# Last chunk of a second MLP: token-major output with the squared-relu part stationary and the weights moving

## The chip, the cores and the metric

The kernel runs on one core of one Trainium2 chip. The metric is the device time of the whole kernel in microseconds (us), as the median of the runs.

## The reference, cut to what matters

The reference computes two transformer blocks over 512 tokens with 1024 features. The change touches only the very end: the last quarter of the second block's MLP, its residual addition, and the final norm.

```
def squared_relu_mlp(u, w_ff1, w_ff2):       # u (512, 1024), w_ff1 (1024, 4096), w_ff2 (4096, 1024)
    hdn = jnp.square(jax.nn.relu(jnp.einsum('bld,df->blf', u, w_ff1)))
    return jnp.einsum('blf,fd->bld', hdn, w_ff2)
...
    h = h + squared_relu_mlp(rmsnorm_2(h, norm_ffn[l]), w_ff1[l], w_ff2[l])
    return rmsnorm_2(h, norm_final)[:, N_META:]
# rmsnorm_2(x, g) = x * rsqrt(mean(x * x, over features) + 1e-6) * g
```

## The kernel before, in words

All activations are held feature-major: `X[p, m, token]` holds feature 128m+p. Column 0 to 15 are meta tokens, 16 to 527 (`META:S2`) the 512 real ones. Every dense product is made of **slabs**: one slab is 128 output features for all 512 tokens, with the weight tile (128x128) stationary and the activations (128x512) moving. For precision each operand is split into a high part in a reduced format and a low part (the remainder), and three products are summed: high by high, high by low, low by high. With eight tiles of the contraction a slab is 24 matmuls. Slabs have a running number `t`.

Five engines work through hand-written streams and meet in counting semaphores:

- **SP** issues the weight loads (`load(p)`, L484 to L491; in the MLP's loop L504). One load brings 1 MB, the raw weights of two slabs, into one of the two halves of `raw`. `load(p)` waits until the low parts of load p-2 were made (`lo_ready`), so two loads ahead are possible.
- **ACT** makes the high part of slab t+2's weights (`wh`, L717 or L666) when slab t is done, because `wh` and `wl` have two slots.
- **DVE** makes the low part (`wl`, L1144 or L1073) and then increments `lo_ready`.
- **TensorE** (PE) starts slab t when `lo_ready` is above t and the result of slab t-2 is evacuated (`evac_done`), because results alternate between two PSUM banks (`products`, L1710; `mlp_chunk`, L1743).

Each MLP has four **chunks** of 1024 hidden features. A chunk is eight slabs of the first product (`j` 0 to 7) and eight of the second (`j` 8 to 15). In the first eight, DVE multiplies the result by the norm's factor `RS` (L1153), makes relu times itself (L1155), ACT copies the high part of the hidden value (L724), and DVE takes the low part (L1158). The second MLP keeps it in `Bh` and `Bl`. In the order of the code, both engines first convert slab t+2's weights and then treat slab t. In the second eight, DVE adds the result to `X` (L1129). Three chunks run in a hardware loop; the last is unrolled (`last`). Its loads come from L531 and L532.

In the last chunk of the second MLP the second eight slabs also prepare the final norm: ACT squares the new `X` (L679) and makes `Y`, `X` times the gain (L745); GpSimd sums the squares (L579), DVE the last one (L1085). TensorE turns `Y` to token-major with four 128x128 transposes for each m (`turn_y`, L1765), into four banks; after m = 3 ACT copies the first halves out (L751). After the last slab come the last square, the sum over partitions by four small matmuls (L2178), mean and epsilon (L1682), square root (L1053), reciprocal (L1684), and the scaling of the four token blocks, the right halves on ACT (L1057) and the left ones on DVE (L1688). SP writes the block of each 128 tokens when both halves are there (L537).

The waits that set the order of loads, and the order of an ACT and DVE step:

```
L488                    sp.wait_ge(lo_ready, loads[p - 2][4] + loads[p - 2][3])
L531            for p in range(second_mlp + 8 * (CHUNKS - 1), len(loads)):
L532                load(p)
L1152                        dve.wait_ge(slab_done, t + 16 * c + 1)
L1748                    pe.wait_ge(lo_ready, t + 16 * c + 1)
L1749                    pe.wait_ge(evac_done, t + 16 * c - 1)
```

Of the kernel before, what the change touches and what calls it, by code (L numbers as in the profile page):

```python
# [32 lines left out]
P = 128  # L33
# [136 lines left out]
def build(nc, d):  # L170
# [21 lines left out]
    with ctx:  # L192
# [152 lines left out]
        y_ready, y_psum, y_copied, y_low, y_high, out_done = (  # L345
            sem("y_ready"), sem("y_psum"), sem("y_copied"), sem("y_low"), sem("y_high"), sem("out_done"))
# [43 lines left out]
        def lr_slab(col):  # L390

            return w_slab(wh, T2_LR % 2, KT)[:, :, col:col + 16]

# [71 lines left out]
        def _(sp):  # L465
# [76 lines left out]
        def _(pool):  # L542
# [103 lines left out]
            add_squares(4, REAL)  # L646
# [3 lines left out]
        def _(act):  # L650
# [51 lines left out]
            def mlp_chunk(which, c, last):  # L702
                t0, n0, p0 = MLPS[which]
                w = width(which)
                for j in range(16):
# [16 lines left out]
                    if j < 8:  # L722
                        act.wait_ge(f_ready, staged(n0) + 8 * c + j)
                        act.activation(HIDDEN[which][0][:, j, 0:w], F[:, (n0 + j) % 2, 0:w], ACT.Copy)\  # L724
                           .then_inc(hi_split, 1)
                    elif last:
                        m = j - 8
                        act.wait_ge(evac_done, t + 16 * c + 1)
                        square(2 if which == ONE else 4, m, which)
                        if which == ONE:  # L730

                            x = X[:, m, META:S2]
                            if m >= 2:
                                act.wait_ge(ss2_done, m - 1)
                            else:
                                act.wait_ge(gain2_ready, 1)
                            act.activation(SQ2[:, m % 2, :], x, ACT.Square, scale=vecT[:, G_FIN + m:G_FIN + m + 1])\
                               .then_inc(sq2_ready, 1)
                            act.activation(Bh[:, m, META:S2], x, ACT.Copy, scale=gain2[:, m:m + 1])\
                               .then_inc(hi_split, 1)  # L740
                            if m == 0:
                                act.activation(Bh[:, :, 0:META], meta2, ACT.Copy).then_inc(meta_hi, 1)
                        else:

                            act.activation(Y[:, m, :], X[:, m, META:S2], ACT.Copy,  # L745
                                           scale=vecT[:, G_FIN2 + m:G_FIN2 + m + 1]).then_inc(y_ready, 1)
                            if m == 4:

                                act.wait_ge(y_psum, 4)
                                for a in range(4):  # L750
                                    act.activation(ON[:, a, 0:512], ps[:, Y_BANKS[a], :], ACT.Copy)\  # L751
                                       .then_inc(y_copied, 1)
# [3 lines left out]
            def mlp(which):  # L756
                with act.Fori(0, CHUNKS - 1) as c:
                    mlp_chunk(which, c, False)
                mlp_chunk(which, CHUNKS - 1, True)
# [292 lines left out]
            act.wait_ge(ms_ready, 5)  # L1052
            act.activation(r_tok, r_tok, ACT.Sqrt).then_inc(sqrt_ready, 1)  # L1053
            act.wait_ge(rstd_ready, 5)
            act.wait_ge(y_psum, KT)
            for a in range(4):
                act.activation(ON[:, a, 512:1024], ps[:, Y_BANKS[a], :], ACT.Copy, scale=r_tok[:, a:a + 1])\  # L1057
                   .then_inc(y_high, 1)
# [3 lines left out]
        def _(dve):  # L1062
# [69 lines left out]
            def mlp_chunk(which, c, last):  # L1132
                t0, n0, p0 = MLPS[which]
                w = width(which)
                for j in range(16):
# [24 lines left out]
                    else:  # L1160
                        add_residual(t + 16 * c, t, j - 8, which)
                        if last:
                            m = j - 8
                            if m == KT - 1:
                                add_square(2 if which == ONE else 4, m, which)
                            if which == ONE:

                                if m == KT - 1:
                                    dve.wait_ge(sq2_ready, KT)
                                    dve.wait_ge(ss2_done, m)  # L1170
                                    dve.wait_ge(meta_sum, 1)
                                    dve.tensor_tensor(SS2[:, META:S2], SS2[:, META:S2], SQ2[:, m % 2, :], ALU.add)\
                                       .then_inc(ss2_done, 1)
                                dve.wait_ge(hi_split, N2_MIX + m + 1)
                                dve.scalar_tensor_tensor(out=Bl[:, m, META:S2], in0=X[:, m, META:S2],
                                                         scalar=gain2[:, m:m + 1], in1=Bh[:, m, META:S2],
                                                         op0=ALU.mult, op1=ALU.subtract).then_inc(act_ready, 1)
                                if m == 0:
                                    dve.wait_ge(meta_hi, 1)
                                    dve.tensor_tensor(Bl[:, :, 0:META], meta2, Bh[:, :, 0:META], ALU.subtract)\  # L1180
                                       .then_inc(meta_split, 1)
# [3 lines left out]
            def mlp(which):  # L1185
                with dve.Fori(0, CHUNKS - 1) as c:
                    mlp_chunk(which, c, False)
                mlp_chunk(which, CHUNKS - 1, True)
# [492 lines left out]
            dve.wait_ge(stat_done, 5)  # L1681
            dve.tensor_scalar(r_tok, ps[:, 7, 0:4], 1.0 / DM, EPS, ALU.mult, ALU.add).then_inc(ms_ready, 1)  # L1682
            dve.wait_ge(sqrt_ready, 5)
            dve.reciprocal(r_tok, r_tok).then_inc(rstd_ready, 1)  # L1684
            dve.wait_ge(rstd_ready, 5)
            dve.wait_ge(y_copied, 4)
            for a in range(4):
                dve.tensor_scalar(ON[:, a, 0:512], ON[:, a, 0:512], r_tok[:, a:a + 1], None, ALU.mult)\  # L1688
                   .then_inc(y_low, 1)
# [3 lines left out]
        def _(pe):  # L1693
# [49 lines left out]
            def mlp_chunk(which, c, last):  # L1743

                t0, n0, _ = MLPS[which]
                for j in range(1, 16 if last else 17):
# [9 lines left out]
                    if last and which == REAL and j >= 9:  # L1756
                        turn_y(j - 9)

            def turn_y(m):

                pe.wait_ge(y_ready, m + 1)
                if m == 4:
                    pe.wait_ge(y_copied, 4)
                for a in range(4):
                    mm = pe.transpose(ps[:, Y_BANKS[a], (m % 4) * P:(m % 4 + 1) * P], Y[:, m, a * P:(a + 1) * P],  # L1765
                                      ident[:, :])
                mm.then_inc(y_psum, 1)

            def mlp(which):
# [5 lines left out]
                mlp_chunk(which, CHUNKS - 1, True)  # L1775
# [400 lines left out]
            pe.wait_ge(ss_done, 8 * 4)  # L2176
            for a in range(4):
# [27 lines left out]
```

## Time and profile before

| | |
|---|---|
| median of 3 runs | 1458.56 us (1457.64 to 1458.94) |
| profiled execution, its own time | 1457.75 us |
| its span, first to last instruction | 1456.0 us |
| mean granted TensorE clock | 0.998 of full speed |
| TensorE busy | 1440.0 us, 99% |
| VectorE (DVE) busy | 776.1 us, 53% |
| ScalarE (ACT) busy | 503.8 us, 35% |
| GpSimd (POOL) busy | 79.1 us, 5% |
| moved by DMA | 130.58 MB, mean 90 GB/s |

The profiled execution has a span and, outside of it, 1.75 us of start and end. Times in rows are counted from the span's start. An engine with a low share of busy time can still be waited for: what counts is what ends each wait of the engine that bounds. PE's weight loads (PEld) run beside its matmuls, and the duration of one matmul in a row is longer than the distance from one to the next, because they are pipelined.

### The profile page before, as it was taken

To read this page: it belongs to the slowest core of one execution; us is meant where nothing else is said; L and a number is where in the kernel's file an instruction comes from. 1 tells how busy PE (TensorE), PEld (TensorE's weight loads), DVE (VectorE), ACT (ScalarE), POOL (GpSimd) and SP (SyncE) were. 2 spreads that over 40 slices of the span, in tenths; PEclk is the share of its full clock that TensorE was granted. 3 is DMA by queue.
4 is the path that set the end of the run, shared out by engine and by line. 5 is a ranking of instruction groups with operands and counts; after the bars stand their busy time and mean duration, and the time that the engine had idled before them with its cause. 6 is when DMAs were issued, how large, how long until landed. Compare 5 with 4: busy or idle time off the path is not lost.

```text
span 1456.0 us, 18718 instructions
## 1 busy us (share of the span) xinstructions
PE 1440.0 (99%) x7726; PEld 1161.2 (80%) x7726; DVE 776.1 (53%) x971; ACT 503.8 (35%) x705; POOL 79.1 (5%) x101
## 2 busy tenths in 40 slices
PE   8999999999999999999999999999999999999997
PEld 7887778777888888888878987777888888888885
DVE  5535433666665354453556787555756345353442
ACT  5224532554433122231343444343442222122233
POOL 4000000000110000000031210000010000000001
PEclk9999999999999999999999999999999999999999
DMA  5223122111233223222323222232233223223321
GB/s 177 87 89 107 59 86 88 59 59 52 93 96 101 93 86 109 93 86 91 112 81 92 74 66 87 75 100 87 87 96 107 87 90 112 86 86 97 105 87 58
DMA packets 125349, 130.58 MB, mean 90 GB/s; under 512 B 2282, under 2 KB 122452, under 8 KB 125284
## 3 DMA queue, kind: packets, MB, share of 16 engines
q1 hardware_dynamic: 124756, 129.12, 27.5%
q8 instruction: 49, 0.80, 0.2%
q10 hardware_dynamic: 528, 0.52, 0.1%
q14 instruction: 16, 0.13, 0.0%
HBM read 126.75 MB, written 2.10 MB: 88 GB/s over the span
## 4 chain that ended last, share of the span: by engine, by line
PE 96%; DVE 2%; ACT 1%; DMA 0%; issue 0%; ACTq 0%; SPq 0%; DVEq 0%
PE ps L1710 85%; PE ps L1706 4%; PE ps L1963 1%; PE ps L1990 1%; PE ps L1976 1%; PE ps L2079 1%; DVE wl L1144 0%; PE ps L1867 0%; DMA arena<-in_norm_mix_g 0%; PE ps L1843 0%; PE ps L1908 0%; PE ps L1887 0%; PE ps L2161 0%; PE ps L1926 0%; DVE wl L1073 0%
## 5 line engine op out<-in xcount | busy, mean ns | idle before, releaser
L1710 PE MATMUL ps<-Ah,wh 128*128 128x512 f32 x1008 | 401.4, 398 | 2.4 <-DVE wl L1234 2.1
L1710 PE MATMUL ps<-Al,wh 128*128 128x512 f32 x1008 | 398.5, 395 | 0.0
L1710 PE MATMUL ps<-Ah,wl 128*128 128x512 f32 x1008 | 396.7, 394 | 0.0
L1710 PE MATMUL ps<-Bh,wh 128*128 128x512 f32 x800 | 317.0, 396 | 0.2 <-issue 0.2
L1710 PE MATMUL ps<-Bl,wh 128*128 128x512 f32 x800 | 316.4, 395 | 0.0
L1710 PE MATMUL ps<-Bh,wl 128*128 128x512 f32 x800 | 314.6, 393 | 0.0
L717 ACT ACTIVATE wh<-raw 128x1024 fp32r<-128x1024 f32 x124 | 131.2, 1058 | 290.3 <-PE ps L1710 290.3
L1144 DVE TENSOR_TENSOR wl<-raw,wh 128x1024 fp32r<-128x1024 f32 x124 | 156.0, 1258 | 139.4 <-ACT wh L717 138.9
L1710 PEld LDWEIGHTS ps<-Ah,wh 128*128 128x128 f32 x1008 | 189.4, 188 | 49.9 <-DVE wl L1234 2.8
L1710 PEld LDWEIGHTS ps<-Ah,wl 128*128 128x128 f32 x1008 | 189.6, 188 | 43.2
L1710 PEld LDWEIGHTS ps<-Al,wh 128*128 128x128 f32 x1008 | 189.2, 188 | 42.3 <-issue 0.5
L666 ACT ACTIVATE wh<-raw 128x1024 fp32r<-128x1024 f32 (+2 forms) x129 | 120.4, 933 | 215.3 <-PE ps L1710 205.0
L1710 PEld LDWEIGHTS ps<-Bh,wh 128*128 128x128 f32 x800 | 150.3, 188 | 38.0 <-issue 1.4
L1710 PEld LDWEIGHTS ps<-Bh,wl 128*128 128x128 f32 x800 | 150.5, 188 | 34.2
L1710 PEld LDWEIGHTS ps<-Bl,wh 128*128 128x128 f32 x800 | 150.1, 188 | 34.0 <-issue 0.2
L1073 DVE TENSOR_TENSOR wl<-raw,wh 128x1024 fp32r<-128x1024 f32 (+2 forms) x129 | 142.4, 1104 | 36.2 <-ACT wh L666 35.7
L1129 DVE TENSOR_TENSOR X<-X,ps 128x512 f32<-128x512 f32 x64 | 44.0, 687 | 162.0 <-PE ps L1710 162.0
L1109 DVE TENSOR_TENSOR arena<-ps,RS 128x512 f32<-128x512 f32 (+2 forms) x59 | 40.7, 690 | 88.6 <-PE ps L1710 83.2
L724 ACT ACTIVATE Ah<-F 128x512 fp32r<-128x512 f32 x32 | 20.2, 632 | 85.6 <-DVE F L1155 85.6
L724 ACT ACTIVATE Bh<-F 128x512 fp32r<-128x512 f32 x32 | 20.2, 632 | 85.6 <-DVE F L1155 85.6
L1153 DVE TENSOR_TENSOR F<-ps,RS 128x512 f32<-128x512 f32 x64 | 43.8, 685 | 4.1 <-PE ps L1710 4.1
L1155 DVE SCALAR_TENSOR_TENSOR F<-F 128x512 f32<-128x512 f32 x64 | 44.3, 692 | 2.2
(261 smaller groups left out, 1047.3 us busy)
## 6 DMA issues: line engine op xcount, KB each, us to landing
raw<-in_w_in SPq DMA_DIRECT2D x38, 1024.0 KB, 5.2
raw<-in_w_ff SPq DMA_DIRECT2D x32, 1024.0 KB, 5.3
raw<-in_w_mlp_in SPq DMA_DIRECT2D x16, 1024.0 KB, 5.3
raw<-in_w_mlp_out SPq DMA_DIRECT2D x16, 1024.0 KB, 5.1
raw<-in_w_out SPq DMA_DIRECT2D x8, 1024.0 KB, 5.2
arena<-in_x SPq DMA_DIRECT2D x4, 512.0 KB, 6.4
raw<-in_w_up_sb SPq DMA_DIRECT2D x2, 1024.0 KB, 4.9
raw<-in_w_pool_out SPq DMA_DIRECT2D x4, 512.0 KB, 3.5
```

The source lines that it names most:

```text
L666: act.activation(w_slab(wh, t % 2, kt), raw_slab(t), ACT.Copy).then_inc(hi_ready, 1)
L717: act.activation(w_slab(wh, t % 2, KT), raw_half((p0 + i) % 2, j % 2, KT, 2), ACT.Copy)\
L724: act.activation(HIDDEN[which][0][:, j, 0:w], F[:, (n0 + j) % 2, 0:w], ACT.Copy)\
L1073: dve.tensor_tensor(w_slab(wl, t % 2, kt), raw_slab(t), w_slab(wh, t % 2, kt), ALU.subtract)\
L1109: dve.tensor_tensor(tokens(dst, kind), dense_psum(t, kind)[0:rows], tokens(scale, kind), ALU.mult)\
L1129: dve.tensor_tensor(X[:, m, META:S2], X[:, m, META:S2], dense_psum(ps_t, kind), ALU.add)\
L1144: dve.tensor_tensor(w_slab(wl, t % 2, KT), raw_half((p0 + (j + 2) // 2) % 2, j % 2, KT, 2), w_slab(wh, t % 2, KT), ALU.subtract).then_inc( ...
L1153: dve.tensor_tensor(f, dense_psum(t, which), RS[:, 0:w], ALU.mult).then_inc(evac_done, 1)
L1155: dve.scalar_tensor_tensor(out=f, in0=f, scalar=0.0, in1=f, op0=ALU.max, op1=ALU.mult)\
L1706: last = pe.matmul(dense_psum(t_ps, ALL)[:, half, :], a[:, k, :], b[:, o0 + k, half * HALF2:(half + 1) * HALF2], start=start, stop=stop)
L1710: last = pe.matmul(dense_psum(t_ps, kind), a[:, k, :], b[:, o0 + k, col0:col0 + S1], start=start, stop=stop)
L1963: pe.matmul(ps[:, 2 + b, 0:nk], qb[rows, hp, n * P:(n + 1) * P], kb[rows, hp, 0:nk], start=True, stop=False)
```

## The change

The eight slabs of the second product in the last chunk of the second MLP become eight **groups** that produce token-major output: group g is token block a = g % 4 and the half g // 4 of the output features. The high and low parts of the hidden values (`Bh`, `Bl`; 128 features by 128 tokens) are stationary, and the second weights (128x512) move. The residual enters PSUM by four transposes of `X` at the start of each group (`is_transpose`, without ending the accumulation), so the group's result is the final `x` of 128 tokens by 512 features.

- For this the whole second weight block of the chunk (1024x1024) must be there as high and low parts at once: `W2h`, `W2l`. They and `late` lie in the memory that `arena` occupied; none of `arena` is in use any more then. `late` holds `raw2`, **one** buffer for 1 MB of raw weights, and `g_row`, the gain broadcast to all partitions.
- SP loads the second weights in four loads of 256 columns into `raw2`, interleaved with the four loads of the first weights: load 0, `g_row`, W2 0, load 1, wait, W2 1, load 2, wait, W2 2, load 3, wait, W2 3. Each wait is for the low parts of the W2 load before (`w2_lo`).
- In each of the eight steps of the first product ACT and DVE convert 128 columns of W2, after the work on the hidden value.
- The final norm: for each group ACT squares the PSUM result and accumulates along the row (`y_sum`). DVE multiplies the left halves (g below 4) by the gain into `ON`. For the right halves it adds both sums, ACT takes the root, DVE the reciprocal and multiplies; ACT scales the left half. `ON` lies in `raw`. GpSimd's sum, `Y`, `turn_y` and the four small matmuls are gone.
- The first MLP keeps its last chunk as it was; the code for it only loses its `which` conditions.

The diff, cut to its core:

```
-        arena = sb("arena", [P, AR])
+        with nc.sbuf_tensor("arena", [P, AR], F32) as arena:
+            pass
+        W2h, W2l = sb("W2h", [P, KT, DM], F32R), sb("W2l", [P, KT, DM], F32R)
+        late = sb("late", [P, 3 * DM])
...
-        Y = region(0, 8, S1)
-        ON = region(4096, 4, DM)
-        Y_BANKS = (1, 3, 4, 5)
+        raw2, g_row = late[:, 0:2 * DM], late[:, 2 * DM:3 * DM]
+        ON = raw[:, :, :].rearrange("p a b -> p (a b)").rearrange("p (a b) -> p a b", a=4)
         X_BANKS = (2, 3, 4, 6, 7)
         X_ON_ACT, X_ON_DVE = (1, 2, 4, 5, 7), (0, 3, 6)
-        r_tok = stat[:, 4, 0:4]
+        y_sum, y_eps, r_tok = stat[:, 0, 0:8], stat[:, 1, 0:4], stat[:, 4, 0:4]
...
+        T_TOK = T2_MLP + 16 * (CHUNKS - 1) + 8
+
+        def raw2_half(i):
+
+            return raw2.rearrange("p (k n) -> p k n", k=KT)[:, :, i % 2 * P:(i % 2 + 1) * P]
+
+        def w2_slab(w, i):
+
+            return w[:, :, i * P:(i + 1) * P]
...
-            for p in range(second_mlp + 8 * (CHUNKS - 1), len(loads)):
-                load(p)
+            for i in range(4):
+                load(second_mlp + 8 * (CHUNKS - 1) + i)
+                if i == 0:
+                    sp.dma_start(g_row, d["norm_final_2"].rearrange("(o n) -> o n", o=1).to_broadcast([P, DM]))\
+                      .then_inc(g_landed, 16)
+                else:
+                    sp.wait_ge(w2_lo, 2 * i)
+                w2 = d["w_ff2_2"][0][(CHUNKS - 1) * DM:CHUNKS * DM, i * 256:(i + 1) * 256]
+                sp.dma_start(raw2.rearrange("p (k n) -> p k n", k=KT), w2.rearrange("(k p) n -> p k n", p=P))\
+                  .then_inc(w2_landed, 16)
 
             for a in range(4):
-                sp.wait_ge(y_low, a + 1)
-                sp.wait_ge(y_high, a + 1)
+                sp.wait_ge(y_left, a + 1)
+                sp.wait_ge(y_right, a + 1)
...
-            add_squares(4, REAL)
...
+            def mlp_tokens():
+                for j in range(8):
+                    t = T_TOK - 8 + j
+                    if j < 6:
+                        convert(t + 2)
+                    act.wait_ge(f_ready, staged(N2_HID) + 8 * (CHUNKS - 1) + j)
+                    act.activation(Bh[:, j, 0:S1], F[:, (N2_HID + j) % 2, 0:S1], ACT.Copy).then_inc(hi_split, 1)
+                    act.wait_ge(w2_landed, 16 * (j // 2 + 1))
+                    act.activation(w2_slab(W2h, j), raw2_half(j), ACT.Copy).then_inc(w2_hi, 1)
+                for g in range(8):
+                    a, t = g % 4, T_TOK + g
+                    act.wait_ge(slab_done, t + 1)
+                    if g >= 2:
+                        act.wait_ge(y_sq, g - 1)
+                    act.activation(SQ[:, g % 2, 0:S1], dense_psum(t, REAL), ACT.Square,
+                                   accum_out=y_sum[:, g:g + 1]).then_inc(y_sq, 1)
+                    if g >= 4:
+                        r = r_tok[:, a:a + 1]
+                        act.wait_ge(y_ms, a + 1)
+                        act.activation(r, r, ACT.Sqrt).then_inc(y_sqrt, 1)
+                        act.wait_ge(y_rstd, a + 1)
+                        act.activation(ON[:, a, 0:S1], ON[:, a, 0:S1], ACT.Copy, scale=r).then_inc(y_left, 1)
...
+            def mlp_tokens():
+                for j in range(8):
+                    t, n = T_TOK - 8 + j, N2_HID + j
+                    if j < 6:
+                        convert(t + 2)
+                    f = F[:, n % 2, 0:S1]
+                    dve.wait_ge(slab_done, t + 1)
+                    dve.tensor_tensor(f, dense_psum(t, REAL), RS[:, 0:S1], ALU.mult).then_inc(evac_done, 1)
+                    dve.wait_ge(evac_done, t + 1)
+                    dve.scalar_tensor_tensor(out=f, in0=f, scalar=0.0, in1=f, op0=ALU.max, op1=ALU.mult)\
+                       .then_inc(f_ready, 1)
+                    dve.wait_ge(hi_split, N2_HID + 8 * (CHUNKS - 1) + (j + 1))
+                    dve.tensor_tensor(Bl[:, j, 0:S1], f, Bh[:, j, 0:S1], ALU.subtract).then_inc(act_ready, 1)
+                    dve.wait_ge(w2_hi, j + 1)
+                    dve.tensor_tensor(w2_slab(W2l, j), raw2_half(j), w2_slab(W2h, j), ALU.subtract).then_inc(w2_lo, 1)
+                dve.wait_ge(g_landed, 16)
+                for g in range(8):
+                    a, t = g % 4, T_TOK + g
+                    if g < 4:
+                        dve.wait_ge(y_sq, g + 1)
+                        dve.tensor_tensor(ON[:, a, 0:S1], dense_psum(t, REAL), g_row[:, 0:S1], ALU.mult)\
+                           .then_inc(evac_done, 1)
+                        dve.tensor_scalar(y_eps[:, a:a + 1], y_sum[:, a:a + 1], 1.0 / DM, EPS, ALU.mult, ALU.add)\
+                           .then_inc(y_eps_ready, 1)
+                    else:
+                        r = r_tok[:, a:a + 1]
+                        dve.wait_ge(y_eps_ready, a + 1)
+                        dve.wait_ge(y_sq, g + 1)
+                        dve.tensor_scalar(r, y_sum[:, g:g + 1], 1.0 / DM, y_eps[:, a:a + 1], ALU.mult, ALU.add)\
+                           .then_inc(y_ms, 1)
+                        dve.wait_ge(y_sqrt, a + 1)
+                        dve.reciprocal(r, r).then_inc(y_rstd, 1)
+                        dve.wait_ge(y_rstd, a + 1)
+                        dve.scalar_tensor_tensor(out=ON[:, a, S1:DM], in0=dense_psum(t, REAL), scalar=r,
+                                                 in1=g_row[:, S1:DM], op0=ALU.mult, op1=ALU.mult).then_inc(y_right, 1)
+                        dve.wait_ge(y_right, a + 1)
+                        dve.sem_inc(evac_done, 1)
...
-                    if last and which == REAL and j >= 9:
-                        turn_y(j - 9)
-
-            def turn_y(m):
-
-                pe.wait_ge(y_ready, m + 1)
-                if m == 4:
-                    pe.wait_ge(y_copied, 4)
-                for a in range(4):
-                    mm = pe.transpose(ps[:, Y_BANKS[a], (m % 4) * P:(m % 4 + 1) * P], Y[:, m, a * P:(a + 1) * P],
-                                      ident[:, :])
-                mm.then_inc(y_psum, 1)
+
+            def mlp_tokens():
+                hh, hl = HIDDEN[REAL]
+                for j in range(1, 8):
+                    full_slab(T_TOK - 8 + j, Ah, Al, 0, REAL)
+                for g in range(8):
+                    half, a, t = g // 4, g % 4, T_TOK + g
+                    out, tok = dense_psum(t, REAL), slice(a * P, (a + 1) * P)
+                    pe.wait_ge(evac_done, t - 1)
+                    for m in range(4):
+                        pe.matmul(out[:, m * P:(m + 1) * P], X[:, 4 * half + m, META + a * P:META + (a + 1) * P],
+                                  ident[:, :], is_transpose=True, start=(m == 0), stop=False, skip_group_check=True)
+                    pe.wait_ge(w2_lo, 4 * half + 4)
+                    cols = slice(half * S1, (half + 1) * S1)
+                    for k in range(KT):
+                        if g == 0:
+                            pe.wait_ge(act_ready, N2_HID + 8 * (CHUNKS - 1) + (k + 1))
+                        for i, (x, w) in enumerate(((hh, W2h), (hl, W2h), (hh, W2l))):
+                            mm = pe.matmul(out, x[:, k, tok], w[:, k, cols], start=False,
+                                           stop=(k == KT - 1 and i == 2), skip_group_check=True)
+                    mm.then_inc(slab_done, 1)
...
-            pe.wait_ge(ss_done, 8 * 4)
-            for a in range(4):
-                mm = pe.matmul(ps[:, 7, a:a + 1], SS[:, a * P:(a + 1) * P], ones[:, 0:1], start=True, stop=True)
-            mm.then_inc(stat_done, 1)
-            turn_y(KT - 1)
```

## Rows read from the trace of the kernel before

**Rows 1.** The page: busy time (share) xinstructions; the chain by engine.

```profile
PE 1440.0 (99%) x7726; PEld 1161.2 (80%) x7726; DVE 776.1 (53%) x971; ACT 503.8 (35%) x705; POOL 79.1 (5%) x101
...
PE 96%; DVE 2%; ACT 1%; DMA 0%; issue 0%; ACTq 0%; SPq 0%; DVEq 0%
```

**Rows 2.** Chain in order of time, the end: start us, us, what.

```profile
1438.41 0.44 PE ps L1765 x4
1438.85 5.58 PE ps L1710 x24
...
1444.46 0.70 DVE X L1129
...
1445.18 0.64 ACT SQ L679
...
1445.84 0.70 DVE SS L1085
...
1446.59 1.07 PE ps L2178 x8
...
1447.68 0.17 DVE stat L1682
...
1447.87 0.21 ACT stat L1053
...
1448.11 0.19 DVE stat L1684
...
1448.32 0.69 ACT arena L1057
```

**Rows 3.** Timeline of DVE, first step: start, us, what, [idle before <-releaser].

```profile
1359.51 1.23 DVE L1144 TENSOR_TENSOR wl<-raw,wh 128x1024 fp32r<-128x1024 f32 x1 [4.40 <-ACT wh L717]
1360.65 0.69 DVE L1153 TENSOR_TENSOR F<-ps,RS 128x512 f32<-128x512 f32 x1
1361.37 0.69 DVE L1155 SCALAR_TENSOR_TENSOR F<-F 128x512 f32<-128x512 f32 x1
1362.77 0.69 DVE L1158 TENSOR_TENSOR Bl<-F,Bh 128x512 fp32r<-128x512 f32 x1 [0.70 <-ACT Bh L724]
1365.01 1.23 DVE L1144 TENSOR_TENSOR wl<-raw,wh 128x1024 fp32r<-128x1024 f32 x1 [1.55 <-ACT wh L717]
```

**Rows 4.** Timeline of ACT, conversions when slabs 0 and 3 are done.

```profile
1358.42 1.06 ACT L717 ACTIVATE wh<-raw 128x1024 fp32r<-128x1024 f32 x1 [4.56 <-PE ps L1710]
...
1375.04 1.06 ACT L717 ACTIVATE wh<-raw 128x1024 fp32r<-128x1024 f32 x1 [1.19 <-PE ps L1710]
```

**Rows 5.** Timeline of DVE, step 7.

```profile
1397.28 0.69 DVE L1153 TENSOR_TENSOR F<-ps,RS 128x512 f32<-128x512 f32 x1 [0.47 <-PE ps L1710]
...
1400.35 1.23 DVE L1144 TENSOR_TENSOR wl<-raw,wh 128x1024 fp32r<-128x1024 f32 x1 [0.26 <-ACT wh L717]
```

**Rows 6.** Line 800, squares with accumulation: ns min/median/max, first and last start.

```profile
L800 ACT ACTIVATION_READ_ACCUMULATOR SQ<-arena x4: 184/186/188, 19.4 to 25.3; 128x1 f32 x4
```

**Rows 7.** Line 537, the output DMAs: issue ns, first and last start; landing.

```profile
L537 SPq DMA_DIRECT2D out<-arena x4: 350/441/1138, 1449.1 to 1450.9; - x4
...
DMA to landing us min/median/max: 2.7/3.8/4.8
```

**Rows 8.** Line 490, weight loads from 1350 to 1370.

```profile
L490 SPq DMA_DIRECT2D raw<-in_w_ff x2: 368/368/368, 1355.1 to 1366.3; - x2
...
DMA to landing us min/median/max: 5.4/5.4/5.4
```

**Rows 9.** Stretch 6 to 14: length, busy by engine, PEclk, DMA share, GB/s.

```profile
6.00:14.00 8.00, 6.65 (x47) 5.89 (x48) 5.51 (x8) 5.80 (x9) 6.97 (x16) 1.00 1.10 349
```

**Rows 10.** Timeline of TensorE, its first dense matmul.

```profile
10.73 0.50 PE L1710 MATMUL ps<-Ah,wh 128*128 128x512 f32 x1 [1.35 <-DVE wl L1234]
```

**Rows 11.** Stretches at the end, as rows 9.

```profile
1448.00:1449.00 1.00, 0.14 (x2) 0.00 (x0) 0.85 (x3) 0.76 (x3) 0.00 (x0) 0.90 0.00 0
1449.00:1450.00 1.00, 0.00 (x0) 0.00 (x0) 1.00 (x3) 1.00 (x3) 0.00 (x0) 0.50 0.09 37
```

More of the change, by code:

```diff
@@ L344, in build @@
         silu_tanh, silu_done = sem("silu_tanh"), sem("silu_done")
-        y_ready, y_psum, y_copied, y_low, y_high, out_done = (
-            sem("y_ready"), sem("y_psum"), sem("y_copied"), sem("y_low"), sem("y_high"), sem("out_done"))
+        w2_landed, w2_hi, w2_lo, g_landed = sem("w2_landed"), sem("w2_hi"), sem("w2_lo"), sem("g_landed")
+        y_sq, y_low, y_eps_ready, y_ms, y_sqrt, y_rstd = (
+            sem("y_sq"), sem("y_low"), sem("y_eps_ready"), sem("y_ms"), sem("y_sqrt"), sem("y_rstd"))
+        y_left, y_right, out_done = sem("y_left"), sem("y_right"), sem("out_done")
         def dense_psum(t, kind):
@@ L728, in mlp_chunk @@
                         act.wait_ge(evac_done, t + 16 * c + 1)
[L729 to L742, printed above, removed]
-                        else:
-                            act.activation(Y[:, m, :], X[:, m, META:S2], ACT.Copy,
-                                           scale=vecT[:, G_FIN2 + m:G_FIN2 + m + 1]).then_inc(y_ready, 1)
-                            if m == 4:
-                                act.wait_ge(y_psum, 4)
-                                for a in range(4):
-                                    act.activation(ON[:, a, 0:512], ps[:, Y_BANKS[a], :], ACT.Copy)\
-                                       .then_inc(y_copied, 1)
+                        square(2, m, which)
+                        x = X[:, m, META:S2]
+                        if m >= 2:
+                            act.wait_ge(ss2_done, m - 1)
+                        else:
+                            act.wait_ge(gain2_ready, 1)
+                        act.activation(SQ2[:, m % 2, :], x, ACT.Square, scale=vecT[:, G_FIN + m:G_FIN + m + 1])\
+                           .then_inc(sq2_ready, 1)
+                        act.activation(Bh[:, m, META:S2], x, ACT.Copy, scale=gain2[:, m:m + 1])\
+                           .then_inc(hi_split, 1)
+                        if m == 0:
+                            act.activation(Bh[:, :, 0:META], meta2, ACT.Copy).then_inc(meta_hi, 1)
                     if j >= 7:
@@ L758, in mlp @@
                     mlp_chunk(which, c, False)
-                mlp_chunk(which, CHUNKS - 1, True)
+                if which == ONE:
+                    mlp_chunk(which, CHUNKS - 1, True)
+                else:
+                    mlp_tokens()
+            def mlp_tokens():
[20 more added lines that the diff above has]
+                        act.activation(ON[:, a, 0:S1], ON[:, a, 0:S1], ACT.Copy, scale=r).then_inc(y_left, 1)
             act.preload_act_table(ACT.Sqrt)
@@ L1051, in _ @@
             mlp(REAL)
[L1052 to L1055, printed above, removed]
-            for a in range(4):
-                act.activation(ON[:, a, 512:1024], ps[:, Y_BANKS[a], :], ACT.Copy, scale=r_tok[:, a:a + 1])\
-                   .then_inc(y_high, 1)
         @block.vector
@@ L1164, in mlp_chunk @@
                             if m == KT - 1:
[L1165 to L1181, printed above, removed]
+                                add_square(2, m, which)
+                            if m == KT - 1:
+                                dve.wait_ge(sq2_ready, KT)
+                                dve.wait_ge(ss2_done, m)
+                                dve.wait_ge(meta_sum, 1)
+                                dve.tensor_tensor(SS2[:, META:S2], SS2[:, META:S2], SQ2[:, m % 2, :], ALU.add)\
+                                   .then_inc(ss2_done, 1)
+                            dve.wait_ge(hi_split, N2_MIX + m + 1)
+                            dve.scalar_tensor_tensor(out=Bl[:, m, META:S2], in0=X[:, m, META:S2],
+                                                     scalar=gain2[:, m:m + 1], in1=Bh[:, m, META:S2],
+                                                     op0=ALU.mult, op1=ALU.subtract).then_inc(act_ready, 1)
+                            if m == 0:
+                                dve.wait_ge(meta_hi, 1)
+                                dve.tensor_tensor(Bl[:, :, 0:META], meta2, Bh[:, :, 0:META], ALU.subtract)\
+                                   .then_inc(meta_split, 1)
                     if j >= 7:
@@ L1187, in mlp @@
                     mlp_chunk(which, c, False)
-                mlp_chunk(which, CHUNKS - 1, True)
+                if which == ONE:
+                    mlp_chunk(which, CHUNKS - 1, True)
+                else:
+                    mlp_tokens()
+            def mlp_tokens():
[22 more added lines that the diff above has]
+                           .then_inc(y_eps_ready, 1)
+                    else:
+                        r = r_tok[:, a:a + 1]
[10 more added lines that the diff above has]
+                        dve.sem_inc(evac_done, 1)
@@ L1679, in _ @@
             mlp(REAL)
[L1681 to L1689, printed above, removed]
         @block.tensor
@@ L1774, in mlp @@
                     mlp_chunk(which, c, False)
-                mlp_chunk(which, CHUNKS - 1, True)
+                if which == ONE:
+                    mlp_chunk(which, CHUNKS - 1, True)
+                else:
+                    mlp_tokens()
             def turn_x(m):
```

3 lines of the change are left out of this document (removed).

## The prediction

> **What bounds the kernel now.** I read the page's first and fourth parts first: TensorE is busy 99% of the span and makes 96% of the chain that ended last, so time is lost or won only where TensorE waits, or before its first or after its last matmul [rows 1]. Next the chain in order of time at the end. A slab of 24 matmuls takes 5.58 us, four transposes 0.44 us, and the last slab is done at 1444.43; then comes a serial tail through DVE, ACT, DVE, TensorE, DVE, ACT, DVE and ACT to the output DMAs [rows 2]. Span 1456.0, so the tail is 11.57 us. The last question is how much room the helpers have while TensorE runs the eight slabs of the last chunk's first half (slabs 0 to 7; I call the helpers' work after slab j "step j"). Slab 0 is done at 1358.4: ACT converts slab 2, DVE takes its low part, evacuates slab 0, squares, waits for ACT's copy and subtracts, until 1363.46 [rows 3, 4]. Slabs are done every 5.56 us: slab 3 at 1375.0, slab 7 at 1397.28 [rows 4, 5].
>
> **The change part by part.**
>
> *Matmuls.* Still 24 per group, 8 groups, f32r 128x128 by 128x512 with the same order of high and low parts. Which operand is stationary changes neither shape, so 8 x 5.57 us stay. Eight sets of four transposes now stand before the last matmul instead of six (one followed slab 15, one stood in the tail): +2 x 0.44 = +0.88 us [rows 2].
>
> *The tail.* Removed: four rounds over all tokens. New, after the last group: ACT squares 128x512 from PSUM with accumulation, 0.64 us by the square in the chain [rows 2] plus 0.19 for reading the accumulator [rows 6]; DVE's small operation 0.17, sqrt 0.21, reciprocal 0.19 [rows 2]; then DVE's 128x512 with two inputs, 0.69, beside ACT's scaling of the other half, 0.69 [rows 2, 3]; some seven handoffs at 0.03. Together 2.3. Then one output DMA instead of four queued ones. Issued alone the first of before landed in 2.7 us, the last after 4.8 [rows 7]; the first three token blocks are now written 6 us apart under matmuls. After landing 0.3 us remain (1450.9 + 4.8 = 1455.7 against 1456.0). New tail 2.3 + 2.7 + 0.3 = 5.3; bounds 5.1 (if reading the accumulator is hidden) and 7.4 (with 4.8 for the DMA). Saved: 11.57 - 5.3 = 6.3 us. With the transposes: -5.4 us, if nothing else changes.
>
> *ACT and DVE in the first half.* Each step gains one ACT conversion (1.06) and one DVE subtraction (1.14 to 1.23) of W2. DVE's step becomes 1.14 + 0.69 + 0.72 + 0.70 wait for the copy + 0.69, then 0.27 of waiting for W2's high part (0.26 where before a conversion follows the copy on ACT [rows 5]) and 1.23. Started at 1359.51 [rows 3] it ends at 1364.95, and step 1's conversion of slab 3 starts at 1365.01 as before. In steps 0 and 1 nothing is late; w2_lo reaches 2 at 1370.45. Where this cover is gone, it costs the overrun.
>
> *The load queue, where the change decides.* Counted from 24 for slabs 0 and 1: before, load 26 (slabs 4, 5) is issued at 1355.1, load 27 (slabs 6, 7) at 1366.3, and each lands after 5.4 [rows 8]. Now SP's order is load 24, the gain row, W2 pair 0, load 25, **wait w2_lo 2**, W2 pair 1, load 26, **wait w2_lo 4**, W2 pair 2, load 27, **wait w2_lo 6**, W2 pair 3. The waits guard raw2, which is one buffer; but loads 26 and 27 of the first half stand behind them on the same queue. And ACT and DVE, in order, stand behind the conversion of the slab that the load brings: the evacuation of the slab before it too.
>
> How long do two 1 MB loads in a row take? One alone takes 5.4 at most, 5.3 by the page's medians; I take 5.3 [rows 8]. The full queue moved 349 GB/s between 6 and 14 us [rows 9], so 1.05 MB need 3.0 us, and the second lands 3.0 after the first: 5.3 + 3.0 = 8.3. The outputs, of 0.5 MB, show such a queue too: the first lands at 1451.8, the fourth at 1455.7, 1.3 apart [rows 7]. Bounds: 5.8 (both at once) and 10.6 (strictly one after the other).
> The Trainium skill, "DMA: Bandwidth & Descriptors", section "Anatomy of one DMA", gives a fixed part of about 2.0 us plus bytes over 436 GB/s; an estimate from that page is 6.8 for the pair, and the sum by it would be 3.0 us lower. The row of a full queue reading weights stands against it, so I keep 8.3.
>
> The recurrence, in us of the span:
> 1. w2_lo 2 at 1370.45; pair landed 1378.8; ACT conversion, DVE conversion, evacuation of slab 2 (1.06 + 1.14 + 0.69 + handoffs = 2.97): slab 4 starts at 1381.8. TensorE had finished slab 3 at 1375.0: **6.8 idle**.
> 2. DVE finishes step 2: square 0.72, wait for copy 0.70, 0.69, 0.27 and 1.14: 3.5. Step 3, with no wait for TensorE: 1.14 + 0.69 + 0.72 + 0.70 + 0.69 + 0.27 + 1.23 = 5.44. w2_lo 4 at 1390.75. Slab 5 needs slab 3's evacuation, which ends at 1387.1; slab 4 ends at 1387.4, so no wait.
> 3. The same again: pair landed 1399.1, slab 6 starts at 1402.1 (slab 5 ended at 1392.9: **9.2 idle**), w2_lo 6 at 1411.05.
> 4. W2 pair 3 alone: landed 1416.4. DVE, in order, waits for W2's high part (1.06) in step 6, subtracts (1.14), and only then evacuates slab 7, which was done at 1413.2: 0.69, square 0.72, copy 0.70, low part 0.69. The last stationary slice is ready at 1421.5. TensorE, in group 0 since 1413.2, had come to k = 7 at 1418.5: **3.0 idle**.
> Without stalls k = 7 is reached at 1397.28 + 0.44 + 21 x 0.232 = 1402.6. The lateness is 18.9 us, of which two pair times (16.6) are the largest term. From there on the W2 halves are there, and each later group has a whole group's time for its evacuation.
>
> **Sum:** 18.9 - 5.4 = +13.5. The profiled execution took 1457.75 (span 1456.0 and 1.75 around it), so 1471.25. It stands 0.8 under the median of the runs, 1458.56; at the median 1472.1, which I predict.
>
> **Clock.** Before, the granted clock was 1.00 where TensorE had a gap of 1.35 us [rows 9, 10], and fell to 0.50 (1.2 GHz) soon after 1448, when TensorE had done only 1.07 us of chain work since 1444.43 [rows 2, 11]. In idles of 7 and 9 us I expect 0.50. What it costs to come back no row shows; bounds are nothing and the whole following slab at half rate, 5.57. After the first idle, slabs 4 and 5 end at 1392.9 and are wanted at 1402.1: 9.2 us of cover. After the second the cover is the 3.0 idle before k = 7. So I count nothing; 5.57 would show 2.6.
> The Trainium skill, "TensorE: Matmul & The Clock Gate", section "HAM oscillation — how this bites in real kernels", speaks against this change: batches separated by DMA waits each start at half rate. Its rule gives the last rival below.
>
> **The rivals.**
> - *The queue hides it (the other sign).* If loads 26 and 27 landed before 1369.5 and 1380.6 (slabs 2 and 4 done, when ACT asks), only the tail and transposes would count: 1458.56 - 5.4 = 1453.2. For it: one load takes only 5.4 of an 11.1 us pitch, so bandwidth is plentiful [rows 8]. Against: the issue of load 26 cannot precede the end of step 1 on DVE, 1370.45, and TensorE wants slab 4 at 1375.0, of which 2.97 go to conversions and evacuation. It decides from a pair time under 1.5 us, or if step 1 ended some 7 us earlier; no row is near either. Even at the lower bound of 5.8, 14 us are lost.
> - *Queue waits exist but the pair overlaps (5.8):* 2 x 2.5 less: 1467.1. *Strictly serial (10.6):* 4.6 more: 1476.7. Both are sizes of my case.
> - *The clock stays low.* If TensorE ran at half rate through slabs 4, 5 and again through slabs 6, 7 and group 0 up to k = 7: 11.1 us become 22.2, 2 late over the cover; 16.4 become 32.8, 13.4 over. 1472.1 + 15.4 = 1487.5. For it the 0.50 of the tail; against, nothing after such a gap is seen here, while 1.00 in all of the dense stretches speaks for a quick return.
>
> **How the numbers follow.** My case with its sizes 0.89, the hidden queue 0.05, the low clock 0.04, and a partial cover that I do not see, ending near no change, 0.02. A measurement of this kernel can tell 0.2% (2.9 us) from no change. So faster 0.05, same 0.02, slower 0.93. The range runs from 1466.5 (overlapping pair and a tail a little shorter) to 1478 (serial pair or some clock loss).
>
> **What would show it.** In the profile after: the loads of slabs 4 and 6 issued right behind a W2 load, near 1371 and 1391; two idles of TensorE before slabs 4 and 6, ended by DVE, 6.8 and 9.2 us; ACT waiting there for DMA; one idle near 3 us inside group 0; seven groups of 6.0 us after it without gaps; a tail of 5 to 6 us with one output DMA in it; the clock at 0.50 in the idles. Wrong would be: load 26 issued before the end of step 1, no idle of TensorE over 2 us before group 0, gaps between the eight groups, or matmuls slower than 0.232 us apart with W2 moving.

## The result, and the profile after

| | before | after |
|---|---|---|
| median of the runs | 1458.75 us (4 runs, 1457.64 to 1458.96) | 1471.12 us (4 runs, 1470.87 to 1471.39) |
| ratio after to before | | 1.0088, 95% interval 1.0076 to 1.0101 |
| span of the profiled execution | 1456.0 us | 1469.3 us |
| mean granted TensorE clock | 0.998 | 0.995 |

The changed kernel is 12.4 us slower by the medians and 13.3 by the spans. The forecast was 1472.1 (+13.5).

A span also holds what came before the changed part, which differs a little between two executions: DVE's first conversion of the stretch starts at 1359.51 in the kernel before [rows 3] and at 1359.68 in the changed one. Counted from that conversion to the end of the span (called "counted from the first conversion" below), it is 13.1 us: 109.62 against 96.49.

Page of the changed kernel, the lines that answer to [rows 1]: TensorE's work has hardly changed, its share of the chain fell from 96 to 92%, and DVE, ACT and a DMA took the difference.

```profile
PE 1444.0 (98%) x7718; PEld 1163.1 (79%) x7718; DVE 775.7 (53%) x976; ACT 498.2 (34%) x704; POOL 70.2 (5%) x94
...
PE 92%; DVE 3%; ACT 2%; DMA 2%; issue 0%; SPq 0%; DVEq 0%; ACTq 0%
```

Waits of TensorE in the changed kernel from 1350 on (waiter, releaser, us in total, times, longest). Before there was only the 1.7 us before the four small matmuls of the norm.

```profile
PE ps L1769 <- DVE F L1227: 13.5, 2, 6.9
PE ps L1833 <- DVE Bl L1232: 0.4, 1, 0.4
```

Timeline of TensorE, the matmuls that stand behind these waits: slab 4, slab 6, and k = 7 of group 0.

```profile
1381.84 0.77 PE L1769 MATMUL ps<-Ah,wh 128*128 128x512 f32 x1 [6.66 <-DVE F L1227]
...
1401.84 0.76 PE L1769 MATMUL ps<-Ah,wh 128*128 128x512 f32 x1 [6.87 <-DVE F L1227]
...
1420.88 0.49 PE L1833 MATMUL ps<-W2h,Bh 128*128 128x512 f32 x1 [0.35 <-DVE Bl L1232]
```

The chain in order of time shows what DVE had waited for. Read from the top: the low part of W2's second slab, SP's issue of the W2 load, the first weights' load behind it, ACT's and DVE's conversion of slab 4, the evacuation of slab 2. SP waits at L552 for W2's low parts; L554 issues W2's load.

```profile
1369.39 1.24 DVE W2l L1234
1370.64 0.37 SPq L554
1371.01 0.04 issue
1371.05 7.70 DMA raw<-in_w_ff
1378.76 0.02 issue
1378.78 1.06 ACT wh L688
1379.84 0.02 issue
1379.87 1.23 DVE wl L1102
1381.09 0.61 DVE F L1227
...
1389.40 1.24 DVE W2l L1234
1390.65 0.37 SPq L554
1391.02 0.04 issue
1391.06 7.69 DMA raw<-in_w_ff
...
1410.65 5.11 DMA late<-in_w_ff
1415.78 1.07 ACT W2h L782
```

The same load of slabs 4 and 5 was issued at 1355.1 before and landed after 5.4, at 1360.5 [rows 8]. Now it lands at 1378.76, and ACT, which could have converted slab 4 from 1369.5 on, has waited for 9.4 us.

The end of the chain answers to [rows 2]: groups of 0.44 and 5.57 to 5.59 us without gaps, and a shorter tail.

```profile
1457.90 0.44 PE ps L1825 x4
1458.34 5.59 PE ps L1833 x24
...
1463.95 0.70 ACT SQ L788 x2
...
1464.75 0.23 DVE stat L1248
1465.00 0.21 ACT stat L793
...
1465.23 0.17 DVE stat L1251
...
1465.43 0.75 DVE raw L1253
```

The output DMAs of the changed kernel, as [rows 7]: each is alone in the queue now. From the last matmul at 1463.93 to the end of the span at 1469.3 are 5.4 us, against 11.6 before.

```profile
L560 SPq DMA_DIRECT2D out<-raw x4: 332/342/363, 1448.2 to 1466.3; - x4
...
DMA to landing us min/median/max: 2.6/2.6/2.7
```

### The profile page after: what moved, and what is told of

It is laid out like the page before. It is cut to its first block, busy times and chain, and to the rows that moved or that the text cites. A ratio compares the mean times of both kernels' runs of the same rounds, so it can differ in the third digit from the quotient of the medians.

```text
span 1469.3 us, 18685 instructions
## 1 busy us (share of the span) xinstructions
PE 1444.0 (98%) x7718; PEld 1163.1 (79%) x7718; DVE 775.7 (53%) x976; ACT 498.2 (34%) x704; POOL 70.2 (5%) x94
## 4 chain that ended last, share of the span: by engine, by line
PE 92%; DVE 3%; ACT 2%; DMA 2%; issue 0%; SPq 0%; DVEq 0%; ACTq 0%
PE ps L1769 79%; PE ps L1765 4%; PE ps L1833 3%; DMA raw<-in_w_ff 1%; PE ps L2034 1%; PE ps L2061 1%; PE ps L2047 1%; DVE wl L1102 1%; PE ps L2150 1%; DVE W2l L1234 1%; DVE wl L1173 0%; ACT W2h L782 0%; ACT wh L688 0%; DMA late<-in_w_ff 0%; PE ps L1938 0%
## 5 line engine op out<-in xcount | busy, mean ns | idle before, releaser
L1769 PE MATMUL ps<-Ah,wh 128*128 128x512 f32 x1008 | 403.2, 400 | 16.0 <-DVE F L1227 13.5
L1769 PE MATMUL ps<-Bh,wh 128*128 128x512 f32 x736 | 291.3, 396 | 0.2 <-issue 0.2
L1769 PE MATMUL ps<-Bl,wh 128*128 128x512 f32 x736 | 291.1, 395 | 0.0
L1769 PE MATMUL ps<-Bh,wl 128*128 128x512 f32 x736 | 289.4, 393 | 0.0
L739 ACT ACTIVATE wh<-raw 128x1024 fp32r<-128x1024 f32 x110 | 116.4, 1058 | 278.2 <-PE ps L1769 278.2
L1173 DVE TENSOR_TENSOR wl<-raw,wh 128x1024 fp32r<-128x1024 f32 x110 | 138.9, 1262 | 109.4 <-ACT wh L739 108.9
L1102 DVE TENSOR_TENSOR wl<-raw,wh 128x1024 fp32r<-128x1024 f32 (+2 forms) x135 | 149.8, 1109 | 59.1 <-ACT wh L688 58.6
L1769 PEld LDWEIGHTS ps<-Bh,wh 128*128 128x128 f32 x736 | 138.2, 188 | 35.4 <-issue 1.4
L1769 PEld LDWEIGHTS ps<-Bh,wl 128*128 128x128 f32 x736 | 138.4, 188 | 31.3
L1769 PEld LDWEIGHTS ps<-Bl,wh 128*128 128x128 f32 x736 | 138.1, 188 | 31.6 <-issue 0.2
L1357 DVE TENSOR_TENSOR arena<-ps,RS 128x512 f32<-128x512 f32 x16 | 16.1, 1007 | 44.9 <-PE ps L1769 44.9
```

What stands on the lines that cost most here:

```text
L739: act.activation(w_slab(wh, t % 2, KT), raw_half((p0 + i) % 2, j % 2, KT, 2), ACT.Copy)\
L1102: dve.tensor_tensor(w_slab(wl, t % 2, kt), raw_slab(t), w_slab(wh, t % 2, kt), ALU.subtract)\
L1173: dve.tensor_tensor(w_slab(wl, t % 2, KT), raw_half((p0 + (j + 2) // 2) % 2, j % 2, KT, 2), w_slab(wh, t % 2, KT), ALU.subtract).then_inc( ...
L1769: last = pe.matmul(dense_psum(t_ps, kind), a[:, k, :], b[:, o0 + k, col0:col0 + S1], start=start, stop=stop)
```

## The experiments

The theory to test: the loss is the order of SP's queue, that is, loads of the first weights behind waits that guard the one buffer `raw2`. Its rivals: the ACT and DVE work added to each step; the granted clock after the idles; a tail that gains nothing.

**e_inplace: the waits taken away by taking away the buffer.** Raw W2 is loaded into W2l's own memory and the low part is made in place.

```
+        with nc.sbuf_tensor("W2raw", [P, KT, DM], F32) as W2raw:     # the memory that W2l gets next
+            pass
         W2l = sb("W2l", [P, KT, DM], F32R)
...
-                    sp.wait_ge(w2_lo, 2 * i)
-                sp.dma_start(raw2.rearrange("p (k n) -> p k n", k=KT), w2...).then_inc(w2_landed, 16)
+                sp.dma_start(W2raw[:, :, i * 256:(i + 1) * 256], w2...).then_inc(w2_landed, 16)
```

> The raw W2 blocks are loaded into the memory of W2l itself and subtracted in place, so raw2 and SP's three waits are gone; ACT's and DVE's work stays as it is. Queue theory: no idle of TensorE before slabs 4 and 6, none in group 0, load 26 issued near 1355; 18.9 us of lateness go, 1453.2 us. Rival 'the added ACT and DVE work makes the steps late' (5.44 us of a 5.56 us slab on DVE): the idles stay in part, 1460 or more. Rival 'the tail brings nothing': about 1459.4.

Measured: 1452.39 us against 1457.75 of the kernel before on the same chip, ratio 0.9962 (0.9949 to 0.9976). The profile has no wait of TensorE from 1350 on. DVE does each step's work as in the changed kernel; its timeline in step 2 shows the conversion of slab 4 9.4 us earlier, and 0.19 us of slack before it, about all the room that the added work leaves:

```profile
1369.06 1.23 DVE L1247 TENSOR_TENSOR W2l<-W2raw,W2h 128x1024 fp32r<-128x1024 f32 x1 [0.26 <-ACT W2h L795]
1370.47 1.22 DVE L1115 TENSOR_TENSOR wl<-raw,wh 128x1024 fp32r<-128x1024 f32 x1 [0.19 <-ACT wh L701]
```

So the added work costs nothing that can be seen. Buffer and waits together cost 18.8 us by the spans (1469.3 - 1450.5), 18.5 counted from the first conversion, and 17.7 by the medians, each against its own runs of before. The rest of the change gains 5.4. This version beats both kernels.

**e_loads_first: the buffer and its waits stay, only the place in the queue changes.** SP's order becomes W2 0, load 1, load 2, wait, W2 1, load 3, wait, W2 2, wait, W2 3.

```
+            load(p0 + 1)
+            load(p0 + 2)
+            w2_load(1)      # waits for w2_lo 2
+            load(p0 + 3)
+            w2_load(2)      # waits for w2_lo 4
+            w2_load(3)      # waits for w2_lo 6
```

> raw2 stays one buffer with its waits, but load 26 stands ahead of the wait for w2_lo 2 and load 27 ahead of the wait for w2_lo 4. Queue theory: slab 4 and slab 6 start without idle. What is left is W2's own wait: its loads cannot start before the low parts of the pair before, so DVE runs late by steps and the last slice of group 0 is about 4 us late: -5.4 + 4.1 against the kernel before, 1457.4 us (1455 to 1460). Rival 'the single buffer is what costs, wherever the first weights' loads stand': near 1471.

Measured: 1457.90 us (ratio 0.9998, 0.9989 to 1.0008). Slab 4 starts without wait; slab 7 and k = 7 of group 0 wait for 1.0 and 2.6 us, 3.6 in all against some 4 expected:

```profile
1393.57 0.47 PE L1780 MATMUL ps<-Ah,wh 128*128 128x512 f32 x1 [1.02 <-DVE F L1238]
1407.26 0.50 PE L1844 MATMUL ps<-W2h,Bh 128*128 128x512 f32 x1 [2.56 <-DVE Bl L1243]
```

The same waits on the same buffer, with two loads moved ahead of them, give back 12 us or more (12.4 above before against 0.2; 13.6 by the spans, 14.3 counted from the first conversion). The single buffer by itself costs 5.5 by the medians (1457.90 - 1452.39), but its profiled execution reached the first conversion 1.0 us later than that of e_inplace (1360.37 against 1359.35). Counted from there it costs 4.2, close to the 4.1 expected, and takes most, not all, of what the tail gains.

**e_swap: within each pair the load of the first weights goes first.**

```
-                    sp.wait_ge(w2_lo, 2 * i); W2 load i; load i + 1
+                    sp.wait_ge(w2_lo, 2 * i); load i + 1; W2 load i
```

> The waits stay, but within each pair the load of the first weights goes ahead of W2's. Queue theory: load 26 and 27 land 5.2 us after the wait instead of 8.1; W2's pair lands after 8.1 but is wanted only about 9.6 after it. Both idles shrink by 2.9 us (to about 4.0 and 4.2), 1471.1 - 5.8 = 1465.3 us. Rival 'the wait itself or the steps' work costs, not the time of the pair': unchanged, 1471.

Measured: 1467.14 us, ratio 1.0064 (1.0048 to 1.0079): 9.4 above the kernel before on its chip, where the changed kernel is 12.4 above. A gain of about 3 (3.8 by the spans, 1465.5 against 1469.3; 3.5 counted from the first conversion), not 5.8. Two things were mis-sized. The load of the first weights now lands 5.7 and 5.6 us after its issue, not 5.2. The 5.2 was what W2's load took as the first of a pair; a load of the first weights took 5.4 even alone [rows 8]. So slab 4 starts 2.4 us sooner after w2_lo 2 (8.8 instead of 11.2), and slab 6 another 2.5 sooner after slab 4 (17.5 instead of 20.0): 4.9 together, not 5.8. And the idle in group 0 grew to 2.33 us, behind which the clock was low:

```profile
1379.08 0.76 PE L1780 MATMUL ps<-Ah,wh 128*128 128x512 f32 x1 [4.25 <-DVE F L1238]
...
1396.62 0.47 PE L1780 MATMUL ps<-Ah,wh 128*128 128x512 f32 x1 [3.60 <-DVE F L1238]
...
1415.64 0.79 PE L1844 MATMUL ps<-W2h,Bh 128*128 128x512 f32 x1 [2.33 <-DVE Bl L1243]
```

A stretch of e_swap in group 0 (length, busy by engine, granted clock, DMA share, GB/s):

```profile
1416.00:1417.00 1.00, 1.00 (x3) 0.69 (x3) 1.00 (x1) 0.00 (x0) 0.00 (x0) 0.50 0.00 0
```

From k = 7 on, the three matmuls, the four transposes and the 24 matmuls took 1.65 + 0.85 + 5.93 us; at full clock 0.96 + 0.44 + 5.58. That is 1.4 us of clock cost on the path, and 4.9 - 1.4 is the 3.5 measured. From the start of slab 6 to k = 7 it takes 19.0 us here, with slab 6 at a granted clock of 1.00, and 19.0 in the changed kernel, with its first ten matmuls at 0.50: the loads and DVE set this stretch, not TensorE's clock. The direction is the queue theory's; the rival that the pair's time doesn't matter falls.

**e_warm: TensorE kept busy in the idles.** What the matmuls compute is read by nothing.

```
+                    if j in (4, 6):
+                        for _ in range(24):
+                            pe.matmul(ps[:, 6, :], Ah[:, 0, 0:P], Ah[:, 0, 0:S1], start=True, stop=True)
```

> 24 matmuls (128x128 by 128x512) of no use are issued before slab 4 and before slab 6, into a bank that nothing reads; about 5.6 us each, within the idles of 6.9 and 7 us. Queue theory: the clock's cost is covered, the time stays at 1471.1 (within 0.6), and the wait in group 0 grows from 0.4 to about 3 us since slabs 4 to 7 run at full clock. Rival 'the low clock after the idles is on the path': the granted clock stays at 1.00 and 1.7 to 3.4 us are won, 1468 to 1469.5.

Measured: 1472.00 us, ratio 1.0097 (1.0082 to 1.0113); not told apart from the changed kernel's 1.0088. The rival's 1468 to 1469.5 is not seen, though slab 4 ran at a granted clock of 1.00. But the test was weaker than planned: in the second pair the load of the first weights took 8.53 us instead of 7.69, 4.0 us of idle were left before slab 6, and the clock fell there all the same. Group 0 waited for 1.0 us, not for 3.

**e_last_pair: the last W2 pair without wait** (in W2l's memory, as in e_inplace; pairs 0 to 2 as in the changed kernel).

```
+            if i in (3,):
+                return W2raw[:, :, i * 256:(i + 1) * 256]
             return raw2.rearrange("p (k n) -> p k n", k=KT)
```

> The changed kernel with W2's last pair loaded into W2l's own memory, without wait; pairs 0 to 2 go through raw2 with their waits as before. Queue theory: DVE evacuates slab 7 when it is done and group 0's last slice is in time; but the low clock after the second idle has used up this cover, so only the measured 0.4 us are won, 1470.7 us. Rival 'the last pair's wait is worth the 3.0 us that the prediction gave it': 1468.

Measured: 1470.28 us, ratio 1.0079 (1.0066 to 1.0093). Group 0 has no wait any more, and the time is about the changed kernel's. Counted in the traces from w2_lo 2 to the end of group 0, 0.4 us are won (50.8 against 51.2), not 3.0, though a load of 5.1 us left the chain.

**e_warm_last_pair: both.** 24 matmuls of no use before slab 4, 36 before slab 6.

> As e_last_pair, with matmuls of no use in the two idles, 24 before slab 4 and 36 before slab 6 (5.6 and 8.4 us), so that no idle of over 1.5 us is left. Clock theory: granted clock 1.00, slabs 6 and 7 and group 0 at full speed, and with the last pair's wait gone this shows in the end: 2.6 us less than the changed kernel, 1468.5 us; each of the two edits alone gives 0.4 or nothing. Rival 'the clock costs nothing at all': as e_last_pair, 1470.7.

Measured: 1470.19 us, ratio 1.0082 (1.0068 to 1.0096): no gain that can be measured, where 2.6 were expected. The two traces show both halves of why. In the chain, slabs 6 and 7 (48 matmuls) took 13.57 us in e_last_pair, and here 11.36 at a granted clock of 1.00. First e_last_pair, then this kernel:

```profile
1391.70 7.74 DMA raw<-in_w_ff
...
1402.52 13.57 PE ps L1782 x48
```

```profile
1391.53 8.75 DMA raw<-in_w_ff
...
1403.37 11.36 PE ps L1782 x48
```

So the low clock costs 2.2 us, and it is on the path once the last wait is gone. But the load before slab 6 took 8.75 us instead of 7.74, and slab 6 started 1.05 later after w2_lo 2 (0.85 by the times above). From w2_lo 2 to the end of group 0 it takes 49.7 us, 1.5 less than the changed kernel. The spans differ by 1.3 (1469.5 and 1468.2); the medians don't: the runs of either kernel lie up to 2.0 us apart, and the profiled one of e_last_pair is its slowest. So the 2.2 us are a reading of two traces, and no gain in time is shown. In e_warm the same load took 8.53. In both kernels with the extra matmuls, and in neither of the two without (the changed kernel and e_last_pair), one transfer of 0.02 MB on the instruction queue falls into that stretch; whether it is the cause wasn't tried.

**e_late_out: e_inplace, with the four output DMAs held back until all is ready.**

```
+            sp.wait_ge(y_left, 4)
+            sp.wait_ge(y_right, 4)
             for a in range(4):
-                sp.wait_ge(y_left, a + 1)
-                sp.wait_ge(y_right, a + 1)
```

> The kernel without raw2 (e_inplace), but SP waits for all four token blocks before it writes the first, as the kernel before had to. Queue theory: the last of four 0.5 MB writes lands three times 1.3 us later than the one write of before: +3.9 us against e_inplace, 1456.3 us, while the compute part of the tail stays at 2.3 us. Rival 'the tail's gain is in its compute chain and the writes cost little': within 1 us of e_inplace's 1452.4.

Measured: 1456.66 us, ratio 0.9986 (0.9977 to 0.9996). That is 4.3 above e_inplace by the medians of two chips (3.4 when each is taken against its own runs of before), 4.4 by the spans (1454.9 and 1450.5) and 4.0 counted from the first conversion, where 3.9 were expected. The last DMA lands 4.8 us after its issue again:

```profile
L573 SPq DMA_DIRECT2D out<-raw x4: 363/610/1194, 1448.0 to 1449.7; - x4
...
DMA to landing us min/median/max: 2.7/4.0/4.8
```

Of the 6.2 us that the tail gained, some 4 are writes that now lie under matmuls; the rest is the shorter chain of computation (4.7 us from last matmul to first issue before, 2.3 after).

**e_no_residual: e_inplace without the four transposes per group** (the residual addition is left out).

> e_inplace without the four transposes of X at the start of each group, which leaves out the residual addition. If the transposes are on the path at 0.44 us a set: 8 x 0.44 = 3.5 us less than e_inplace, 1448.9 us. Rival 'they hide in TensorE's pipeline or under waits': 1452.4.

Measured: 1449.72 us, ratio 0.9937 (0.9922 to 0.9952). That is 2.7 below e_inplace by the medians of two chips (3.6 by their ratios to before, 2.5 by the spans). The groups' matmuls in its chain are one piece, `1398.10 44.60 PE ps L1843 x192`, 5.575 us a group. In e_inplace the eight groups with their transposes take 48.1 (1397.09 to 1445.18), 3.5 more. The smaller difference of the spans comes from before the stretch: counted from the first conversion it is 3.5 too. The transposes don't hide.

The profiled executions, counted from the first conversion to the end of the span:

| kernel | first conversion starts | from there to the end | against before |
|---|---|---|---|
| before | 1359.51 | 96.49 | |
| changed | 1359.68 | 109.62 | +13.1 |
| e_inplace | 1359.35 | 91.15 | -5.3 |
| e_loads_first | 1360.37 | 95.33 | -1.2 |
| e_swap | 1359.34 | 106.16 | +9.7 |
| e_warm | 1359.36 | 110.34 | +13.9 |
| e_last_pair | 1360.33 | 109.17 | +12.7 |
| e_warm_last_pair | 1360.13 | 108.07 | +11.6 |
| e_late_out | 1359.80 | 95.10 | -1.4 |
| e_no_residual | 1360.36 | 87.64 | -8.9 |

## Why the prediction was right, point by point

- **Where the loss arises.** Right. Both idles stand before slabs 4 and 6, behind the pair of loads; e_inplace and e_loads_first make them vanish in two different ways.
- **The pair of loads.** 8.3 us taken, 8.1 measured (0.37 + 0.04 + 7.70). The rule that the second lands one full-queue transfer behind the first held (2.9 us measured between the landings, 3.0 taken from [rows 9]). The formula in the Trainium skill, "DMA: Bandwidth & Descriptors", section "Anatomy of one DMA", stands there for DMAs issued over GpSimd's path, while these loads are issued by SP; the estimate from it was 6.8 for the pair, and the 8.1 measured decide against using it here.
- **The recurrence.** Slab 4 foreseen at 1381.8, measured 1381.84; slab 6 at 1402.1, measured 1401.84; w2_lo 4 at 1390.75, measured 1390.64. Idles 6.8 and 9.2 foreseen, 6.66 and 6.87 measured. The first is right. The second was foreseen 2.3 too long: slab 4 ran its first nine matmuls at half clock, so slab 5 ended at 1394.97 and not at 1392.9, and slab 6 started 0.3 earlier than foreseen. The end of that idle, which is what counts, is set by the loads.
- **The idle in group 0.** 3.0 foreseen, 0.35 measured. The last slice was foreseen for 1421.5 and k = 7 began at 1420.88. What was wrong is TensorE's arrival, 1420.5 and not 1418.5, again by the low clock (2.2 us by e_last_pair against e_warm_last_pair). The last slice came 0.6 sooner than foreseen.
- **The clock.** The granted clock fell as foreseen and its cost was covered in both places, as the prediction said, but in the second with little to spare: 2.2 us of a cover of some 2.6. No row of before gave this cost, so that it stayed under the cover was not worked out; a cost nearer the upper bound of 5.57 would have shown in the time. The stretches of the changed kernel around the first idle (length, busy by engine, granted clock, DMA share, GB/s):

```profile
1378.00:1380.00 2.00, 0.00 (x0) 0.00 (x0) 0.13 (x1) 1.06 (x1) 0.00 (x0) 0.72 0.04 12
1380.00:1382.00 2.00, 0.16 (x1) 0.19 (x2) 1.97 (x3) 0.00 (x0) 0.00 (x0) 0.50 0.00 0
1382.00:1384.00 2.00, 2.00 (x5) 1.62 (x6) 1.11 (x2) 1.55 (x3) 0.00 (x0) 0.50 0.00 0
1384.00:1386.00 2.00, 2.00 (x6) 1.53 (x6) 1.94 (x2) 0.98 (x2) 0.00 (x0) 0.57 0.00 0
1386.00:1388.00 2.00, 2.00 (x10) 1.64 (x9) 1.72 (x3) 0.22 (x1) 0.00 (x0) 1.00 0.00 0
```

  It came back within slab 4, so the rival of a clock that stays low falls. The Trainium skill's section "HAM oscillation — how this bites in real kernels" (TensorE: Matmul & The Clock Gate) has each batch behind a DMA wait start at half rate. The trace agrees for both idles here (0.50 at 1382 and at 1402); after e_swap's idle of 3.60 us the clock was 1.00, so it does not hold for every one. The rival went further, with half rate through whole slabs. Here the clock shaped the idles and not the end.
- **The tail.** 5.3 foreseen, 5.4 measured. The square with the reading of its accumulator took 0.70 instead of 0.83, the operation on 128x1 0.23 instead of 0.17 and the last product 0.75 instead of 0.69; the DMA 2.6 instead of 2.7.
- **Transposes.** +0.88 foreseen; each set stands in the chain at 0.44, and leaving out all eight won 3.5 us counted from the first conversion.
- **The other sign.** The rival of a hidden queue put the time at 1453.2 for the case without waits. e_inplace is that case, with 1452.4.

## What to carry to other kernels

A wait in a DMA queue holds back everything issued behind it. When new loads with a buffer wait are interleaved with old ones, write down for each old load when it was issued, which wait it now stands behind, and which slab needs it: two loads put ahead of the waits were worth 12 us here. If a block is to be split into a high and a low part, its raw data can land in the memory of the low part, if nothing else uses that memory yet; then neither buffer nor wait is needed. And a cost that is covered by a wait (the low clock, 2.2 us) appears as soon as that wait is removed, so single edits around one wait don't add up.

## What the runs showed of the hardware that was not expected

The length of an idle alone did not tell whether the granted clock fell. In e_swap an idle of 3.60 us left it at 1.00 and one of 2.33 us, 17 us later, was followed by 0.50; in e_loads_first it stayed at 1.00 through 2.56 us. All six idles of over 4 us (4.03 in e_warm, 4.25 in e_swap, 6.66 and 6.87 in the changed kernel, 6.65 and 6.68 in e_last_pair) were followed by 0.50, for some 3 to 5.5 us after the restart. Why the one of 2.33 us was too stays open. Rows of e_loads_first and e_swap around the shorter ones:

```profile
1406.00:1407.00 1.00, 0.00 (x0) 0.00 (x0) 0.48 (x1) 1.00 (x2) 0.00 (x0) 1.00 0.00 0
1407.00:1408.00 1.00, 0.74 (x3) 0.63 (x4) 0.74 (x2) 0.43 (x1) 0.00 (x0) 1.00 0.00 0
```

```profile
1394.00:1396.00 2.00, 0.00 (x0) 0.00 (x0) 1.36 (x2) 0.61 (x1) 0.00 (x0) 1.00 0.81 256
1396.00:1398.00 2.00, 1.38 (x6) 1.20 (x7) 1.27 (x3) 0.77 (x2) 0.00 (x0) 1.00 0.00 0
```
